# A normalised split operand and wide products in the two-layer part of an fp32 kernel

## The reference, cut to what matters

```python
def rms_norm_2(x, g):
    y = x * lax.rsqrt(jnp.mean(x * x, axis=-1, keepdims=True) + EPS)
    return y * g
def swiglu(h, w_gate_up, w_down):
    g, u = jnp.split(h @ w_gate_up, 2, axis=-1)
    return (jax.nn.silu(g) * u) @ w_down
def hybrid_mixer(h, w_in, b_gate, conv_w, w_conv_out, w_pg, b_pg, pool_scale, w_pool_out, w_o):
    b_g, c_g, v, p, gates = jnp.split(h @ w_in, [1024, 2048, 3072, 4096], axis=-1)
    y_a = (b_g * causal_depthwise_conv(c_g * v, conv_w)) @ w_conv_out
    y_p = pool_mixer(p, w_pg, b_pg, pool_scale) @ w_pool_out   # means over 2, 4, 8, 16 positions
    g_a, g_p = jnp.split(jax.nn.sigmoid(gates + b_gate), 2, axis=-1)
    return (g_a * y_a + g_p * y_p) @ w_o
for l in range(2):
    x = x + 0.5 * rms_norm_2(swiglu(rms_norm_2(x, ffn1_pre[l]), ...), ffn1_post[l])
    x = x + rms_norm_2(hybrid_mixer(rms_norm_2(x, mix_pre[l]), ...), mix_post[l])
    x = x + 0.5 * rms_norm_2(swiglu(rms_norm_2(x, ffn2_pre[l]), ...), ffn2_post[l])
```

## Time and profile before

| | |
|---|---|
| three runs | 1861.85, 1861.85, 1862.13 us; median 1861.85 |
| the profiled execution | 1861.95 us; its span 1860.1 us; mean granted clock 0.998 |
| TensorE busy | 1822.5 us, 98% (weight loads 1720.6 us, 92%) |
| VectorE busy | 1436.2 us, 77% |
| ScalarE busy | 972.5 us, 52% |
| GpSimd busy | 204.1 us, 11% |
| the chain that ended last | PE 82%, DVE 10%, ACT 3%, POOL 2% |
| costliest lines | L243 724.1 us (x313), L234 597.3 us (x313), L261 to L263 on `x_split` 541.0, 537.0, 537.0 us |

### The profile page before, as it was taken

The page is one execution under the profiler, slowest core; times in us unless marked ns, Lnnn a source line. Parts: engine busy times, 40 slices in busy tenths (PEclk is TensorE's granted clock), DMA queues, the critical chain, the costliest instruction groups (busy, mean ns, idle before and its releaser), DMA issues.

```text
span 1860.1 us, 31793 instructions
## 1 busy us (share of the span) xinstructions
PE 1822.5 (98%) x13284; PEld 1720.6 (92%) x13284; DVE 1436.2 (77%) x1707; ACT 972.5 (52%) x1174; POOL 204.1 (11%) x160
## 2 busy tenths in 40 slices
PE   7999999999999999999999999999999999999997
PEld 7889999999999998899999998889888999999887
DVE  7987996598998578758875797759775896578774
ACT  6356665385765455544453555545553445445542
POOL 2001321000432030002200010001000320001000
PEclk9999999999999999999999999999999999999999
DMA  7324555434555545564454455554555445445551
GB/s 291 131 105 159 184 183 201 182 137 181 182 204 181 204 159 183 204 221 146 164 199 175 159 188 197 192 193 167 196 204 204 159 174 191 157 161 205 199 207 67
DMA packets 46789, 334.67 MB, mean 180 GB/s; under 512 B 5184, under 2 KB 5568, under 8 KB 6464
## 3 DMA queue, kind: packets, MB, share of 16 engines
q1 hardware_dynamic: 46512, 332.20, 49.3%
q0 software_dynamic: 144, 0.52, 0.1%
HBM read 331.65 MB, written 1.05 MB: 179 GB/s over the span
## 4 chain that ended last, share of the span: by engine, by line
PE 82%; DVE 10%; ACT 3%; POOL 2%; DMA 1%; issue 1%; SPq 0%; DVEq 0%; ACTq 0%
PE psum L277 24%; PE psum L282 12%; PE psum L261 11%; PE psum L263 11%; PE psum L262 11%; PE psum L303 6%; DVE w_lo L243 4%; PE psum L310 3%; POOL scratch L1748 1%; DMA w_raw<-stream_in 1%; POOL x_resid L393 1%; ACT w_hi L234 1%; POOL scratch L1745 1%; DVE scratch L330 1%; PE psum L599 1%
## 5 line engine op out<-in xcount | busy, mean ns | idle before, releaser
L234 ACT ACTIVATE w_hi<-w_raw 128x2048 fp32r<-128x2048 f32 x313 | 597.3, 1913 | 416.3 <-PE psum L263 157.6
L243 DVE TENSOR_TENSOR w_lo<-w_raw,w_hi 128x2048 fp32r<-128x2048 f32 x313 | 724.1, 2316 | 37.8 <-ACT w_hi L234 37.7
L261 PE MATMUL psum<-x_split,w_hi 128*128 128x256 f32 x1896 | 541.0, 285 | 13.9 <-DVE x_split L425 10.5
L262 PE MATMUL psum<-x_split,w_hi 128*128 128x256 f32 x1896 | 537.0, 283 | 0.0
L263 PE MATMUL psum<-x_split,w_lo 128*128 128x256 f32 x1896 | 537.0, 283 | 0.0
L261 PEld LDWEIGHTS psum<-x_split,w_hi 128*128 128x128 f32 x1896 | 364.4, 192 | 15.4 <-issue 14.8
L262 PEld LDWEIGHTS psum<-x_split,w_hi 128*128 128x128 f32 x1896 | 364.5, 192 | 0.5
L263 PEld LDWEIGHTS psum<-x_split,w_lo 128*128 128x128 f32 x1896 | 364.4, 192 | 0.0
L277 PE MATMUL psum<-x_split,w_hi 128*128 128x512 f32 x1088 | 341.7, 395 | 0.0
L277 PE MATMUL psum<-h_split,w_hi 128*128 128x512 f32 x816 | 256.3, 395 | 0.0
L282 PEld LDWEIGHTS psum<-x_split,w_lo 128*128 128x128 f32 x1088 | 204.4, 188 | 48.3
(11 more groups left out here) (249 smaller groups left out, 2412.3 us busy)
## 6 DMA issues: line engine op xcount, KB each, us to landing
w_raw<-stream_in SPq DMA_DIRECT2D x313, 1024.0 KB, 4.8
x_resid<-x_in SPq DMA_DIRECT2D x1, 1024.0 KB, 7.1
y_out<-x_resid SPq DMA_DIRECT2D x4, 256.0 KB, 2.5
scratch<-mask_in SPq DMA_DIRECT2D x1, 768.0 KB, 11.1
scratch<-ev_in SPq DMA_DIRECT2D x1, 512.0 KB, 9.7
scratch<-inv_in POOLq DMA_DIRECT2D x1, 512.0 KB, 6.6
params<-par_in SPq DMA_DIRECT2D x1, 247.0 KB, 7.3
matrices<-mat_in SPq DMA_DIRECT2D x1, 192.0 KB, 8.9
```

The lines of the kernel that those rows point to most:

```text
L234: act.activation(w_hi[:, n % RING, :], raw[:, n % RAWS, :], ACT.Copy).then_inc(hi_ready, 1)
L243: dve.tensor_tensor(w_lo[:, n % RING, :], raw[:, n % RAWS, :], w_hi[:, n % RING, :].bitcast(F32), ALU.subtract).then_inc(lo_ready, 1)
L261: pe.matmul(dst, w_hi[:, c.slot, b:b + P], src[:, k0 + k, 0, :], start=opens, stop=False)
L262: pe.matmul(dst, w_hi[:, c.slot, b:b + P], src[:, k0 + k, 1, :], start=False, stop=False)
```

## The change

All of it is in the two-layer part.

- **More wide chunks.** `WIDE` now gives the first wide chunk per stage: upA from 5 (as before), upB from 6, pool_in from 3, and all of cv and gates. These 17 chunks of each mixer were narrow.
- **An operand that holds the norm.** `SCALED` gives the chunks that read it: upA and upB from 7, pool_in from 3, all of cv and gates. `scale_dve` (VectorE, eight instructions) makes x times gain times `inv_rms`; `scaled_hi` (ScalarE, four copies of 128 x 512) rounds it; `scaled_lo` (VectorE, four subtractions) takes the rest. It lies in free parts of the scratch (up stages) and of `h_split` (mixer). In each such chunk TensorE waits for the rest, two k at a time.
- **Eviction.** A scaled wide chunk ends with the sum; there is no multiply by `inv_rms` behind it. A newly wide chunk of the mixer has a ScalarE copy of its right halves in front.
- **Where the new work stands.** In the mixer: `scale_dve` after `w_lo` of bg's chunk 2, `scaled_lo` after that of chunk 3, ahead of `unroot_dve`; `scaled_hi` on ScalarE after bg's chunk 2. In the up stages: four scalings behind chunk 2's work and four behind chunk 3's, two subtractions behind chunk 4's and two behind chunk 5's; `unroot_dve` moves from chunk 3 to behind chunk 5's.

```diff
+WIDE = {"upA": 5, "upB": 6, "pool_in": 3, "cv": 0, "gates": 0}
+SCALED = {"upA": 7, "upB": 7, "pool_in": 3, "cv": 0, "gates": 0}
...
-LAYER = [("upA", FF2, 2 * FF2 - NARROW), ("downA", 12, 7), ("bg", 4, 4), ("pool_in", 4, 4), ("cv", 8, 8),
-         ("gates", 8, 8), ("conv_out", 4, 4), ("pool", 1, 4), ("pool_out", 4, 4),
-         ("w_o", 4, 4), ("upB", FF2, 2 * FF2 - NARROW), ("downB", 12, 7)]
+LAYER = [events("upA", FF2), ("downA", 12, 7), ("bg", 4, 4), events("pool_in", 4), events("cv", 8),
+         events("gates", 8), ("conv_out", 4, 4), ("pool", 1, 4), ("pool_out", 4, 4),
+         ("w_o", 4, 4), events("upB", FF2), ("downB", 12, 7)]
...
-        self.wide = phase in WIDE and n >= NARROW
-        self.event = E0[phase] + n + layer * LAYER_EVENTS + (n - NARROW if self.wide else 0)
+        self.wide = phase in WIDE and n >= WIDE[phase]
+        self.scaled = phase in SCALED and n >= SCALED[phase]
+        self.event = E0[phase] + n + layer * LAYER_EVENTS + (n - WIDE[phase] if self.wide else 0)
         self.bank = self.event % BANKS
+        assert not self.wide or self.bank % 2 == 0, phase
...
-                dve.wait_ge(up_right, wide_count(c))
-                dve.tensor_tensor(dst, ps[:, c.bank:c.bank + 2, 0:T], S(ACC + 2 * c.slot, 2),
+                dve.wait_ge(up_right, WIDE_COUNT[c.number])
+                dve.tensor_tensor(dst, ps[:, c.bank:c.bank + 2, 0:T], right_halves(c),
                                   ALU.add).then_inc(pair_taken, 2)
+                if c.scaled:
+                    return
...
+        def right_halves(c):
+            return S({"pool_in": GP, "cv": GP, "gates": PIN}.get(c.phase, ACC) + 2 * c.slot, 2)
+        def copy_right(act, c):
+            act.activation(right_halves(c), ps[:, c.bank:c.bank + 2, T:2 * T], ACT.Copy).then_inc(up_right, 1)
+        def scaled_operand(phase):
+            return hs[:, 16:24, :, :] if phase in HYBRID else xn_up[:, :, :, :]
+        def scaled_words(phase):
+            at = H(16, 2 * KT) if phase in HYBRID else S(XN, 2 * KT)
+            return at.rearrange("p (k a) t -> p k a t", a=2)
+        def scale_dve(dve, tr, phase, gain, ks):
+            for k in ks:
+                dve.scalar_tensor_tensor(out=scaled_words(phase)[:, k, 1, :], in0=x[:, k, :],
+                                         scalar=gain[:, k:k + 1], in1=rinv[:, :],
+                                         op0=ALU.mult, op1=ALU.mult).then_inc(*tr["xn"].one())
+        def scaled_hi(act, tr, phase, gs, l):
+            for g in gs:
+                act.wait_ge(*tr["xn"].count(2 * g + 2, l))
+                act.activation(scaled_operand(phase)[:, 2 * g:2 * g + 2, 0, :],
+                               scaled_words(phase)[:, 2 * g:2 * g + 2, 1, :], ACT.Copy)\
+                   .then_inc(*tr["xhi"].one())
+        def scaled_lo(dve, tr, phase, gs, l):
+            for g in gs:
+                dve.wait_ge(*tr["xhi"].count(g + 1, l))
+                both = scaled_operand(phase)[:, 2 * g:2 * g + 2, :, :]
+                dve.tensor_tensor(both[:, :, 1, :], scaled_words(phase)[:, 2 * g:2 * g + 2, 1, :],
+                                  both[:, :, 0, :].bitcast(F32), ALU.subtract).then_inc(*tr["xlo"].one())
...
+        def whole(pe, c, tr, hooks={}):
+            if c.scaled:
+                multiply_wide(pe, c, (c.bank, c.bank + 1), scaled_operand(c.phase), 0, KT, True, True,
+                              lambda k: tr["xlo"].count(k // 2 + 1, c.layer), hooks=hooks)
...
+                if phase in SCALED and at in (3, 4):
+                    scaled_hi(act, pre, phase, (0, 1) if at == 3 else (2, 3), l)
...
-                    if at == 3 and post is not None:
-                        unroot_dve(dve, *post)
+                if phase in SCALED and at in (2, 3):
+                    scale_dve(dve, pre, phase, gain, range(0, 4) if at == 2 else range(4, 8))
+                if phase in SCALED and at in (4, 5):
+                    scaled_lo(dve, pre, phase, (0, 1) if at == 4 else (2, 3), l)
+                if at == 5 and post is not None:
+                    unroot_dve(dve, *post)
...
+                if g == 2:
+                    scaled_hi(act, N["normM"], "pool_in", G4, l)
...
             for at in range(8):
                 c = Chunk("cv", at, l)
                 act.wait_ge(chunk_done, c.number + 1)
+                copy_right(act, c)
                 refill_hi(act, c)
...
                     take_scaled(dve, chunk0, S(YA + 2 * chunk0.n, 2))
                 take_scaled(dve, c, S(YA + 2 * g, 2))
                 refill_lo(dve, c)
+                if g == 2:
+                    scale_dve(dve, N["normM"], "pool_in", gains2("mpre", l), range(KT))
                 if g == 3:
+                    scaled_lo(dve, N["normM"], "pool_in", G4, l)
                     unroot_dve(dve, PN["postA"], l)
```

More of the change, by code:

```diff
@@ L39, with events @@
 LEVELS = 8
-NARROW = 5
 AWAKE = 6
 MEAN_AT = 4
-WIDE = ("upA", "upB")
+WIDE = {"upA": 5, "upB": 6, "pool_in": 3, "cv": 0, "gates": 0}
+SCALED = {"upA": 7, "upB": 7, "pool_in": 3, "cv": 0, "gates": 0}
+def events(name, count):
+    return name, count, count + max(0, count - WIDE[name]) if name in WIDE else count
 FIRST = [("ev_in", 13, 13), ("ev_out", 4, 4), ("up0", FF1, FF1), ("down0", 12, 7),
@@ L98 @@
 EV_GK, EV_Q = 2, 3
-PRE, ACC, GEL, HID, HB = 0, 8, 16, 20, 24
+PRE, ACC, GEL, HID, HB, XN = 0, 8, 16, 20, 24, 24
+HYBRID = ("bg", "pool_in", "cv", "gates")
+SCALED_NORMS = ["normA", "normM", "normB"]
 YA, PIN, GA, GP, PRE2, ACC2, UU, INV = 0, 8, 16, 24, 32, 38, 41, 44
@@ L167, in chunks @@
     return [Chunk(phase, n, layer) for n in range(done, count)]
+WIDE_COUNT, UNSCALED_COUNT = {}, {}
+_w, _u = 0, 0
+for _layer, _stages in [(0, FIRST)] + [(_l, LAYER) for _l in range(LAYERS2)]:
+    for _name, _nc, _ in _stages:
+        for _n in range(_nc):
+            _chunk = Chunk(_name, _n, _layer)
+            _w += _chunk.wide
+            _u += _chunk.wide and not _chunk.scaled
+            WIDE_COUNT[_chunk.number], UNSCALED_COUNT[_chunk.number] = _w, _u
 def program(nc, x_in, stream, par1_in, par2_in, ev_const, mask_const, mats, inv_in, out):
@@ L185, in program @@
         hs = sb("h_split", [P, FF1, 2, T], F32R)
+        with nc.sbuf_tensor("scratch_first", [P, XN, T], F32), \
+                nc.sbuf_tensor("scaled_split", [P, KT, 2, T], F32R) as xn_up:
+            pass
         scr = sb("scratch", [P, SCR, T])
@@ L439, in pre_pe, with whole_pe @@
                     pe.wait_ge(lo_ready, c.number + 1)
-                    whole(pe, c, hooks={mean_at: lambda: mean_pe(pe, tr, summed, l), 2: mean})
+                    whole(pe, c, tr, hooks={mean_at: lambda: mean_pe(pe, tr, summed, l), 2: mean})
                     done = 3
-                whole_pe(pe, ph, n, l, done)
-        def whole_pe(pe, ph, n, l, done=0):
+                whole_pe(pe, ph, n, tr, l, done)
+        def whole_pe(pe, ph, n, tr, l, done=0):
             for c in chunks(ph, n, l, done):
@@ L743, in up_tracks @@
             return {k: Signal(sem(f"{name}_{k}_ready"), 2 * m if k == "taps" else m) for k in names}
-        def wide_count(c):
-            return (WIDE.index(c.phase) + 2 * c.layer) * (FF2 - NARROW) + c.n - NARROW + 1
         def scaled(c):
-            if c.wide:
-                return up_scaled, wide_count(c)
-            return taken(c.event)
+            if c.wide and not c.scaled:
+                return up_scaled, UNSCALED_COUNT[c.number]
+            return taken(c.last)
         def up_act(act, phase, n, tr, func, conv, pre, l, final=None):
@@ L769, in taps @@
                 w, b = conv
-                act.wait_ge(*taken(c.event))
+                act.wait_ge(*taken(c.last))
                 for t in range(2):
@@ L1378, in hybrid_act @@
                 act.wait_ge(chunk_done, c.number + 1)
+                if c.wide:
+                    copy_right(act, c)
                 refill_hi(act, c)
@@ L1775, in hybrid_dve @@
                     pooled_lo(g - 1)
-                dve.wait_ge(*taken(c.event))
+                dve.wait_ge(*taken(c.last))
                 src = S(PIN + 2 * g, 2)
@@ L2102, in _ @@
                 more = l + 1 < LAYERS2
-                up_dve(dve, "upA", FF2, U["upA"], None, N["normA"], l, (PN["postB"], l - 1) if l else (PN["final"], 0))
+                up_dve(dve, "upA", FF2, U["upA"], None, N["normA"], gains2("nextA", l - 1) if l else final_pre, l,
+                       (PN["postB"], l - 1) if l else (PN["final"], 0))
                 last = out_dve(dve, "downA", 3, O["downA"], HB, l)
```

28 lines of the change are left out of this document (16 added, 12 removed).

## The result

The changed kernel takes 1879.76 us (median of four runs, 1879.65 to 1881.58), the kernel before 1861.99 beside it: a ratio of 1.0096, 95% interval 1.0079 to 1.0114. It is slower, by 17.8 us; 13.0 were forecast. The profiled execution took 1879.75 us, its span is 1877.9.

What follows compares the result with a forecast made beforehand. TensorE, busy 98% of the span, bounds the kernel: chunks times chunk length, plus stalls. Mixers 10.0, up phases 2.6 and upB's later widening 0.4 make 13.0 us on 1861.95: 1875 us, range 1864 to 1881.

Steps and rivals of the forecast that it cites:

- The waits: TensorE in cv, ahead of its first four chunks, waits for VectorE's evictions: 2.5, 2.8, 3.5 and 0.5 us.
- The multiply that goes: Up phases: 60 chunks lose a VectorE multiply of 0.71 us each; 0 us on the path, since VectorE idles there.
- Only the two slots: Rival, mixers: VectorE's new work hides completely and only the bank shortage costs, 0.6 us per mixer; 1866, chance 14 of 100.
- Faster: Rival: VectorE's freed time lets evictions follow chunks at once, and both 1.24 us waits go; 1853, chance 8 of 100.
- three signs of being wrong: cv runs without waits, GpSimd's residual does not move, or the clock shows 0.5 in the mixers.
- The mixers: Late VectorE evictions and two slots in place of four make each mixer 5.0 us longer, 10.0 for two.
- The lower end for this step: VectorE's first pool step after the mean, put at 888.8, comes at 886.5 if GpSimd hid 2 us more.
- The rival's mechanism: Mixers: TensorE's clock falls in the new waits, 0.9 us per mixer stays; 1877, dearest case 1887; chance 13 of 100.
- v3's start: Start of cv's fourth chunk on TensorE: 915.1 in place of 907.65, 7.45 us lost.
- The up phases: Residual beside wide chunks delays evictions: 2.6 us together, bounds 0 and 5; upB turning wide later adds 0.4.
- The second upA: In upA of the second layer, chunk 9 waits 1.2 us for the banks of chunk 7.
- Each upB: Eviction delay as in upA, one chunk later into wide: 0.7 us per layer, apart from turning wide later.

Runs made afterwards that it cites:

- e6: Changed kernel with only the up phases scaled, upB wide from 5, and the mixers as in the kernel before: 1867.54 us against 1861.86, ratio 1.0027.
- e7: Changed kernel with pool means ahead of the residual, its reciprocal in gates, pool_in and cv's first five chunks narrow, up phases unscaled: 1858.12 us against 1861.86, 0.998.
- e1: Changed kernel with GpSimd's pool means ahead of its residual, and the residual's reciprocal moved from bg to gates: 1868.07 us against 1863.46 for the kernel before, 1.0032.
- e4: Changed kernel with extra matmuls into an unused bank ahead of cv's first (12) and third (10) chunks, so TensorE works in the long waits: 1876.82 us.
- e2: Changed kernel with pool_in and the first five chunks of cv narrow and unscaled, all new VectorE work left in place: 1874.06 us, ratio 1.0062.
- e8: Same as e7, but with the up phases scaled as in the changed kernel: 1860.55 us (one run).
- after: The changed kernel itself, as against the kernel before: 1879.76 us against 1861.99, ratio 1.0096.
- e3: Changed kernel with up phases unscaled and their reciprocal back behind chunk 3, upB wide from 6, mixers unaltered: 1877.86 us, ratio 1.0081.

## Why the prediction was right, and where its sizes were off

**Right.** The waits stand where they were put, for evictions by VectorE; the residual begins 5.6 us later against the mixer's start (6 forecast); chunks of gates come 5.58 us apart (5.57); VectorE idles 2.01 us in late upA (about 2). The multiply that goes gains nothing (e6), and eleven copies a mixer cost nothing where evictions are on time (e7). Two rivals are out. "Only the two slots" put the delay at nothing, and without the delay each mixer is some 5 us shorter (e1). "Faster" let the spared multiplies pay, and no up phase gained (e6). Of the three signs of being wrong one did come: the clock shows 0.50 in both mixers. It did not carry the loss (e4), but 1.0 us of it.

The time itself lies at the upper end of the forecast's own range (1869 to 1880), and 1.5 of the 4.8 us missed have nothing to do with the change.

**The mixers: 5.0 forecast, 7.1 and 6.05 measured.** Two terms were mis-sized.
- L1836 was put at 888.8; it came at 891.45, less the 1.49 of the first part 889.96. The residual had been priced at its old 7.63 us and took 9.66, with two `w_lo` of VectorE beside it. From the mean's start to L1836 it took 3.35 us where it had taken 5.41, 2.06 made good for the 1.5 assumed, and the residual started 0.3 sooner: 2.03 - 0.3 - 0.56 = 1.2 us late. I had priced GpSimd's blocking for the mean and not for the residual. (The lower end for this step, 2 us less than 888.8, is 886.8 and not 886.5; nothing hangs on it.)
- The clock, which the sum left out: some 1.0 us of the first mixer (e4). The rival's mechanism was real, and its 0.9 per mixer is near the 1.0 to 1.4 measured wherever the clock fell ahead of v2. The sum stands without it: in e4, 5.0 + 1.2 = 6.2 against 6.08 and 6.18.

The waits were forecast at 2.5, 2.8, 3.5 and 0.5 us and were 3.8, 0.9, 3.2 and none in the first mixer: the first is longer by the 1.2, and the slow v0 eats into the second. What counts is v3's start: 7.45 us late by forecast, and measured from the mixer's start 9.6 and 8.5 (8.5 in e4's first).

**What the explanation lacked.** The prediction gave the whole loss to two slots behind a late VectorE. e2 shows that with four slots the delay still leaves 4 to 5 us, since `w_lo`, which VectorE makes behind the late evictions, comes late as well. The wide join without the delay costs 3.3 (e1 against e7), a fall of the clock ahead of v2 in e1 (0.53 at 904 to 906 us) included; without the fall some 2.3.

**The up phases: 2.6 + 0.4 forecast, 3.2 measured** (1.84 + 0.67 + 0.66). The second upA was forecast at 1.2 and waits 1.58; `w_lo` beside the residual took 3.38 us, not 3.0. But this run was a dear one: in e1, e2, e4, e6 and e8, with the same upA and the same 3.38 us, it waits 1.09 and costs 1.34 to 1.36. In after ScalarE had waited 3.02 us for a weight chunk to land (at 1289.91; 1.59 in e4), and VectorE's evictions came 0.5 us later. Each upB was forecast at 0.9 (the 0.7 is stated there without its rows) and cost 0.67.

**The rest** of the 17.8 us, 1.5, is the clock in the first part of the profiled run, for which the prediction had no term. Together: 13.1 + 3.2 + 1.5.

## What to carry to other kernels

Where an engine in a chain of three already runs behind, price new work in its queue by what waits behind it, and count the releases, not the busy time: 43 us of work taken off VectorE bought nothing, and 5.6 us put ahead of one reciprocal cost 4.7 to 7.0 in each mixer. A wide product that saves 0.19 us takes twice the banks, so it belongs where its evictions are on time (gates), not at a join. Before moving such work, look for the step in the slow chain that nobody needs yet: the residual here. Its move behind the means took 4.7 to 7.0 us off each mixer; with the join left narrow and the up phases unscaled too, the loss became a small gain (e7).

## What the runs showed that was not expected

- GpSimd and VectorE block each other whichever goes first: the residual 7.10 us in e1, where it lies in gates, 7.63 before and 9.66 in after; VectorE's four subtractions 2.50 or 5.78.
- The clock's fall does not follow from a wait's length alone: it fell ahead of v2 in after's first mixer (wait 3.21) and not in the second (3.25), but in both of e3's (3.23 each); in e4 it stayed at 1.00 through a wait of 2.43, and in e2 it fell behind one of 2.32. What decides is not shown. The Trainium skill's rule that the prediction named (TensorE: Matmul & The Clock Gate, A second HAM failure mode: psum-queue depth-cycling) agrees with the falls in after in kind, since they stand behind waits for PSUM banks; they took 1.0 of the 17.8 us. e2's stand behind waits for `w_lo`.
- It also fell in the first part (0.50 at 124 to 126 us) in after and e6 and in none of the other profiled runs, whose first part is the same, for some 1.5 us.
